# Token rows of a grouped mixture of experts: gathered by TensorE per block, or scattered to DRAM once per layer and read back

## What is computed

```
e_idx, wts = top-2 experts of the token's best group, weights normalised
dest  = position of each (token, expert) pair in a list that is sorted by
        expert and padded to whole blocks
xs    = h_pad[slot_tok].reshape(n_blocks, BLOCK, D)          # rows of one expert
def block_ffn(args):
    xb, e = args
    return (silu(xb @ w_gate[e]) * (xb @ w_up[e])) @ w_down[e]
ys    = lax.map(block_ffn, (xs, block_e))
out   = zeros(N + 1, D).at[slot_tok].add(ys * slot_w)[:N]
```

## Time and profile before

| | |
|---|---|
| runs | 1494.18, 1494.39, 1498.3 us; median 1494.39 |
| the profiled execution | 1502.44 us, its span 1500.3 us |
| TensorE busy | 1428.7 us, 95% of the span |
| VectorE, ScalarE, Pool busy | 45%, 16%, 7% |
| DMA, mean of the span | 335 GB/s; 409 or 410 in most slices of the expert loops |
| DMA queues | q1 (SyncE) 487.84 MB, 82.5% of 16 engines' span; q0 (Pool) 11.21 MB, 2.3% |
| granted clock, mean | 0.974 |

### The profile page before, as it was taken

One profiled execution on the slowest core, in us unless ns is written; L12 is line 12 of the kernel. 1 busy time (PEld: TensorE's weight loads), 2 busy tenths in 40 slices (PEclk: granted clock), 3 DMA queues, 4 the chain that ended last, 5 costly groups with the idle time before them and its releaser, 6 DMA issues.

```text
span 1500.3 us, 19677 instructions
## 1 busy us (share of the span) xinstructions
PE 1428.7 (95%) x6993; PEld 658.7 (44%) x6994; DVE 682.3 (45%) x1986; ACT 239.8 (16%) x392; POOL 104.6 (7%) x149
## 2 busy tenths in 40 slices
PE   6999998999999999999989999999999999999996
PEld 2777664333333233333347766633333333333333
DVE  2697647333323333343338965553333323233333
ACT  1201322111111011111130122211111101111112
POOL 1071111000000000000002511100000000000000
PEclk9899998999999999999999999889999999999998
DMA  9944558999999985899998265589999999979991
GB/s 335 352 175 151 209 204 322 410 409 410 409 410 410 409 321 223 309 410 410 409 409 331 112 242 210 192 330 393 410 410 409 410 409 410 409 299 409 410 410 72
DMA packets 131317, 501.98 MB, mean 335 GB/s; under 512 B 8635, under 2 KB 8955, under 8 KB 131266
## 3 DMA queue, kind: packets, MB, share of 16 engines
q1 hardware_dynamic: 127056, 487.84, 82.5%
q0 software_dynamic: 3600, 11.21, 2.3%
q10 hardware_dynamic: 626, 2.46, 0.6%
HBM read 495.32 MB, written 7.00 MB: 335 GB/s over the span
## 4 chain that ended last, share of the span: by engine, by line
PE 60%; SPq 25%; DMA 5%; DVE 4%; issue 3%; ACT 2%; PEld 1%; PEldq 1%; ACTq 0%; DVEq 0%
PE ps L414 57%; SPq L380 18%; SPq L376 4%; PE ps L417 3%; DMA ring<-in_w_mod 2%; DMA ring<-in_w_exp_up 2%; SPq L396 1%; SPq L318 1%; PEld ps L414 1%; ACT hT L866 1%; ACT arena L866 1%; ACT L866 0%; SPq L382 0%; DVE stat L1053 0%; PEldq L563 0%
## 5 line engine op out<-in xcount | busy, mean ns | idle before, releaser
L414 PE MATMUL ps<-ring,arena 128*64 128x512 f32 x2816 | 635.7, 599 | 16.9 <-DMA ring<-in_w_exp_up 13.8
L414 PEld LDWEIGHTS ps<-ring,arena 128*64 128x64 f32 x2816 | 194.9, 137 | 404.7 <-issue 356.0
L866 ACT ACTIVATE arena<-ps 128x512 f32<-128x512 f32 (+3 forms) x240 | 129.6, 551 | 1124.8 <-PE ps L414 1033.9
L414 PE MATMUL ps<-arena 64*128 64x288 f32 (+4 forms) x1484 | 296.3, 505 | 12.0 <-DVE arena L1383 4.7
L414 PE MATMUL ps<-hT,ring 128*128 128x288 f32 x1024 | 257.9, 414 | 8.4 <-DVE hT L1127 4.1
L1416 DVE SCALAR_TENSOR_TENSOR xT<-ps,mod,xT 128x256 f32<-128x256 f32 x280 | 133.4, 476 | 267.7 <-PE ps L414 267.7
L414 PEld LDWEIGHTS ps<-hT,ring 128*128 128x128 f32 x1024 | 197.8, 194 | 66.4 <-issue 6.9
L414 PEld LDWEIGHTS ps<-arena 64*128 64x128 f32 (+4 forms) x1484 | 119.6, 161 | 203.0 <-issue 180.2
L1158 DVE SCALAR_TENSOR_TENSOR arena<-arena,wcT 128x256 f32<-128x256 f32 x240 | 123.5, 575 | 1.6
L1450 DVE TENSOR_TENSOR arena<-ps,arena 128x512 f32<-128x512 f32 x35 | 24.2, 692 | 195.9 <-PE ps L414 195.9
L417 PE MATMUL ps<-cst,arena 128*128 128x128 f32 (+5 forms) x533 | 83.0, 289 | 12.2 <-DVE arena L1040 7.2
(11 more groups left out here) (173 smaller groups left out, 628.3 us busy)
## 6 DMA issues: line engine op xcount, KB each, us to landing
ring<-in_w_exp_up SPq DMA_DIRECT2D x128, 1024.0 KB, 18.0
ring<-in_w_exp_down SPq DMA_DIRECT2D x128, 1024.0 KB, 17.7
ring<-in_w_exp_gate SPq DMA_DIRECT2D x64, 1024.0 KB, 17.8
ring<-in_w_mod SPq DMA_DIRECT2D x48, 1024.0 KB, 8.9
arena<-in_w_exp_gate SPq DMA_DIRECT2D x32, 1024.0 KB, 17.1
ring<-in_w_in SPq DMA_DIRECT2D x24, 1024.0 KB, 21.4
big<-in_w_exp_gate SPq DMA_DIRECT2D x16, 1024.0 KB, 18.2
hT<-in_w_exp_gate SPq DMA_DIRECT2D x16, 1024.0 KB, 18.4
```

Of the source, the lines that this page charges most:

```text
L414: return nc.tensor.matmul(out, lhsT, rhs, start=start, stop=stop, skip_group_check=True)
L866: return nc.scalar.activation(out, in_, f, **kw)
```

## The change

- A tensor in DRAM, `block_rows`, of 1664 rows x 1024 is added, and zeroed once, in the first layer, by one Pool DMA of 6.8 MB out of the still zero tile qm. VectorE waits for it before it first writes qm.
- Once per layer, after the row numbers, VectorE casts them to integers (rowi), and Pool issues six indirect DMAs (three token tiles, two experts a token) that put each token's row at its two places. Pool waits until all have landed, and for gt0_done, and then reads block 1's rows with two DMAs of 64 rows x 2 KB. All this stands ahead of the history load, of Pool's waits and drains, and so of `mix_open`.
- In the loop Pool issues the two reads of the next block as soon as TensorE has transposed the rows before them (xg_trans).
- TensorE loses the gather in the loop, ScalarE the copy of its result, VectorE sel, sel1 and their sum. The first block of a layer is still gathered.
- The fourth combining pair goes from the up product, and the third from the gate product, to the place after the transposes of hs, ahead of the down product; their PSUM banks change. VectorE takes them after it has copied the transposed hs. After the last block the old banks and order remain.
- The transposes are in another order: rows first (now after up, waiting for the DMA), then selw, then hs.

```diff
+XROWS = -(-(MAXBLK + 1) * BLK // P) * P
...
-        PAIR_BANKS = ((6, 7), (0, 5), (1, 4), (0, 5))
+        PAIR_BANKS = ((6, 7), (0, 5), (5, 7), (2, 3))
+        LAST_BANKS = ((6, 7), (0, 5), (1, 4), (0, 5))
...
                                 if k == 3:
                                     pe.wait_ge(V.y_copied, nn)
                                     pe.wait_ge(V.selT_copied, nn)
-                                    for j in range(3):
+                                    for j in range(2):
                                         combine(j).then_inc(V.comb_done, 1)
...
-                                if k == 0:
-                                    pe.wait_ge(V.comb_used, taken)
-                                    combine(3).then_inc(V.comb_done, 1)
...
-                            pe.wait_ge(V.sel_ready, nn)
-                            pe.reg_add(taken, taken, 1)
+                            pe.reg_add(got, got, 32)
+                            pe.wait_ge(V.rows_in, got)
+                            transposes(1, xtok).then_inc(V.xg_trans, 1)
+                            pe.wait_ge(V.selw_ready, nn)
+                            pe.reg_add(taken, taken, 2)
                             pe.wait_ge(V.comb_used, taken)
-                            gather().then_inc(V.gathered, 1)
-                            pe.wait_ge(V.h_act, nn)
-                            transposes(4, hs).then_inc(V.trans_done, 1)
-                            pe.wait_ge(V.selw_ready, nn)
                             for t, (t0, m) in enumerate(TILES):
                                 last = tr(ps[:, 6, t0:t0 + m], selw[0:m, t, :], m)
                             last.then_inc(V.selT_done, 1)
-                            pe.wait_ge(V.xrow_copied, nn)
-                            transposes(1, xtok).then_inc(V.xg_trans, 1)
+                            pe.wait_ge(V.h_act, nn)
+                            transposes(4, hs).then_inc(V.trans_done, 1)
+                            for j in range(2, 4):
+                                combine(j).then_inc(V.comb_done, 1)
...
+                v.tensor_copy(rowi[:, :, :], slots[:, :, :]).then_inc(V.rowi_ready, 1)
...
+                if l == 0:
+                    zeros = qm[:, :, :].rearrange("p h w -> p (h w)")
+                    pool.dma_start(xrows.rearrange("(p r) d -> p r d", p=P),
+                                   zeros.unsqueeze(1).to_broadcast([P, XROWS // P, D])).then_inc(rows_zeroed, 16)
...
+                pool.wait_ge(V.h2_copied, 6)
+                pool.wait_ge(V.rowi_ready, 1)
+                for t, (t0, m) in enumerate(TILES):
+                    for k in range(2):
+                        gp.indirect_dma_start(xrows[:, :], bass.IndirectOffsetOnAxis(ap=rowi[0:m, k, t:t + 1], axis=0),
+                                              h2tok[0:m, t, :], None).then_inc(rows_out, 16)
+                pool.wait_ge(rows_out, 96 * (l + 1))
+                pool.wait_ge(V.gt0_done, 1)
+
+                def read_rows(r0):
+                    for nh in range(2):
+                        pool.dma_start(xtok[nh * BLK:(nh + 1) * BLK, :], xrows[bass.ds(r0, BLK), nh * 512:nh * 512 + 512]) \
+                            .then_inc(V.rows_in, 16)
+
+                read_rows(BLK)
...
                 pool.drain().then_inc(mix_open, 1)
+                nb = pool.value_load(nsubi[0:1, E:E + 1], min_val=E, max_val=MAXBLK)
+                with pool.Fori(1, nb) as n:
+                    pool.wait_ge(V.xg_trans, n)
+                    pool.sem_inc(tick, 1)
+                    read_rows(n * BLK + BLK)
```

More of the change, by code:

```diff
@@ L145, in hybrid_step_kernel @@
         nsubi = sb("nsubi", [P, E + 1], i32)
+        rowi = sb("rowi", [P, 2, 3], i32)
+        xrows = nc.dram_tensor("block_rows", (XROWS, D), f32, kind="Internal").ap()
         rtmp = sb("rtmp", [P, KC, NS])
@@ L224, in hybrid_step_kernel @@
         sel = cut("moe", 3, BLK)
-        sel1 = cut("moe", 3, BLK)
         selw = cut("moe", 3, 2 * BLK)
@@ L420, in _ @@
             taken = pe.alloc_register("chunks_taken")
+            got = pe.alloc_register("rows_in_x32")
             for s in range(NSLOT):
@@ L741, in half_products, with combine @@
                     return last
-                def combine(j):
+                def combine(j, banks=PAIR_BANKS):
                     for hf in range(2):
-                        last = mm(ps[:, PAIR_BANKS[j][hf], 0:T], ysb[hf * 64:hf * 64 + 64, j * P:(j + 1) * P],
+                        last = mm(ps[:, banks[j][hf], 0:T], ysb[hf * 64:hf * 64 + 64, j * P:(j + 1) * P],
                                   selT[hf * 64:hf * 64 + 64, :], True, True)
@@ L756, in _ @@
                 pe.reg_mov(nn, 0)
-                pe.reg_mov(taken, 2)
+                pe.reg_mov(taken, 0)
+                pe.reg_mov(got, 0)
                 with pe.Fori(0, E // 2) as e2:
@@ L825, in _ @@
                             last.then_inc(V.down_done, 1)
+                            pe.reg_add(taken, taken, 2)
+                            pe.wait_ge(V.comb_used, taken)
+                            pe.sem_inc(tick, 1)
                 pe.reg_add(nn, nn, 1)
@@ L1427, in _ @@
                     last.then_inc(V.bchain, 1)
-                    dve.wait_ge(V.bchain, n * 3 + 1)
+                    dve.wait_ge(V.bchain, n * 2 + 1)
                     v.tensor_tensor(selw[:, :, :], selw[:, :, :], selw1[:, :, :], ALU.add).then_inc(V.selw_ready, 1)
                     v.tensor_scalar(slots[:, :, :], slots[:, :, :], -float(BLK), None, ALU.add).then_inc(V.bchain, 1)
-                    dve.wait_ge(V.bchain, n * 3 + 2)
-                    for t in range(3):
-                        v.tensor_scalar(sel[:, t, :], iota[:, 0:BLK], slots[:, 0, t:t + 1], None, ALU.is_equal)
-                    for t in range(3):
-                        last = v.tensor_scalar(sel1[:, t, :], iota[:, 0:BLK], slots[:, 1, t:t + 1], None, ALU.is_equal)
-                    last.then_inc(V.bchain, 1)
-                    dve.wait_ge(V.bchain, n * 3 + 3)
-                    v.tensor_tensor(sel[:, :, :], sel[:, :, :], sel1[:, :, :], ALU.add).then_inc(V.sel_ready, 1)
-                    for j in range(3):
+                    for j in range(2):
                         dve.wait_ge(V.comb_done, n * 4 + j + 1)
@@ L1444, in _ @@
                     v.tensor_tensor(hs, ps[:, 2, :], gs, ALU.mult).then_inc(V.gated, 1)
-                    dve.wait_ge(V.comb_done, n * 4 + 4)
-                    take(3)
                     dve.wait_ge(V.up_done, n + 1)
@@ L1452, in _ @@
                     v.tensor_copy(h2T, ps[:, 4, :]).then_inc(V.hT_copied, 1)
+                    for j in range(2, 4):
+                        dve.wait_ge(V.comb_done, n * 4 + j + 1)
+                        take(j)
                     dve.wait_ge(V.selT_done, n + 1)
+                    dve.wait_ge(V.bchain, n * 2 + 2)
                     v.tensor_copy(selT, ps[:, 6, 0:T]).then_inc(V.selT_copied, 1)
@@ L1569, in _ @@
                     pool.dma_start(dstate(rets_v, h), state(h)).then_inc(V.states_stored if i < 2 else V.Sa_stored, 16)
+                if l == 0:
+                    pool.wait_ge(rows_zeroed, 16)
+                pool.wait_ge(V.h2_copied, 6)
[11 more added lines that the diff above has]
+                read_rows(BLK)
                 pool.wait_ge(V.sf_stored, 16)
```

18 lines of the change are left out of this document (8 added, 10 removed).

## The result

The changed kernel takes 1539.8 us (median of 4 runs, 1535.2 to 1544.0) against 1496.4 us for the kernel before beside it (4 runs, 1494.2 to 1503.2): a ratio of 1.0281, 95% interval 1.0235 to 1.0328. The direction is the predicted one. The size is not: 1518 was forecast, and the upper end of the range, 1538, lies 2 us under the first median.

A forecast was written before the change was run, and what follows sets the result against it. The weight stream was taken to bound the kernel except in double experts. Gate delay and reads less TensorE's gain, with 5.0 us of lead spent at the end, gave +12.2 and +12.0, together +24 on 1494.4: 1518 us, range 1504 to 1538.

The forecast's parts named there:

- What bounds the kernel: Expert loop: one expert's weights take 30.7 us, one TensorE block 27.7; TensorE is slower only where an expert has two blocks.
- TensorE's block: Expert loop: gather and moved combining pairs cut a TensorE-paced block from 27.73 to 25.0 us, 2.7 less.
- What that is worth: Double experts only: TensorE's saving gives 9.2 us in the first layer and 3.8 us in the second.
- The reads: Expert loop: each block's 256 KB of rows costs the weight stream 0.8 us, upper end 1.3.
- Which blocks pay: Expert loop: reads cost time in 13 blocks of the first layer and 14 of the second; the others fall in idle stream.
- The scatter: Ahead of `mix_open`: scatter, landing wait and reads open the gate 12 us later in each layer; bounds 7 and 22.
- Hidden: Scratch zeroing, 16.6 us of DMA at 50 to 93 us, is covered; so is block 1's wait of some 2 us.
- C: Half-rate reads in the loop: 1.3 instead of 0.8 us a block, 27 times, +14, 1532 us; chance 0.12.
- rival B: Slow scatter ahead of the gate: 3 us per indirect DMA, gate 22 us late in each layer, 1538 us; chance 0.10.
- A: The forecast itself, gate delay and reads less TensorE's gain: 1518 us; chance 0.66.
- D: No change: the gate opens when it does now and a read costs 0.65 us, 1490 to 1496 us; chance 0.05.
- E: Faster: gate as now, and reads filling gaps between the weights' packets cost the stream nothing, 1473 us; chance 0.04.

The follow-up runs named there:

- pairs_only: The kernel before with only the two combining pairs moved; TensorE still gathers every block, no scratch, scatter or reads: ratio to before 1.0001.
- no_reads: The changed kernel with block rows never read back, Pool raising the semaphore itself; only the first layer is comparable: 477.9 us against 497.4.
- pairs_scatter: The kernel before with the two combining pairs moved, plus zeroing and scatter ahead of the gate, nothing read back: 1509.6 us, ratio to before 1.0081.
- after: The changed kernel itself, against the kernel before: 1539.8 us, ratio 1.0281.
- reads_inter: The changed kernel with block rows read by one DMA over all 128 partitions from a contiguous source, ScalarE's copy restoring order: 1514.8 us, ratio to before 1.0114.
- reads_twice: The changed kernel with each block's rows read a second time into a tile nobody reads: 1584.7 us.
- gate_first: The changed kernel with the scatter, its wait and the first read moved behind Pool's signal mix_open: 1545.8 us.
- before: The kernel without the change: 1496.4 us beside the changed kernel, 1498.0 to 1498.9 beside the experiments.

## Why the prediction was wrong

By its own steps:

- **What bounds the kernel: right.** Weights pace single-block experts; TensorE's saving came back in the double ones and hardly elsewhere. pairs_only and the waits above show it.
- **TensorE's block: right in the sum.** 24.81 against 25.0. In its parts the moved pairs bring 0.2 us (0.4 by my terms, 1.21 + 0.42 - 0.85 - 0.38), and the gather more.
- **What that is worth: a little low.** -9.2 was forecast for the first layer; no_reads minus pairs_scatter gives -12.2 (0.9 of it is a signal that stands earlier, 3.3 instead of 2.4 us before the first product), the pairs another -0.8. I had counted three blocks at TensorE's pace and a part; in no_reads five periods of 24.81 us follow one another (560 to 684 us).
- **The reads: the step that failed.** I took 0.8 us a block, from the earlier trace rows, and 1.3 as the upper end. In single-block experts it is 1.3, and by layers 19.5 us for the first against 10.4 forecast. A read over all partitions costs 0.61 us a block, and 487.6 - 477.9 = 9.7 us in that layer. So the row's 0.8 was somewhat high for the transfer that the row shows (all partitions), and far too low for the one that the change makes (half of them); that 9.7 is near 10.4 is luck, a lower price on more blocks. The prediction also says of the earlier trace rows that Pool's 1.47 MB take no more of the engines than their bytes; the row has 4.4 us of all engines where the bytes at 410 GB/s are 3.6. And the rows travel in packets of 4 KB, 64 a read, not of 2 KB. For the second layer after minus pairs_scatter is +17.2, against 11.2 - 3.8 = 7.4 forecast; 12.4 of it go with whole-width reads (after minus reads_inter), and 2.4 are a later signal (3.6 instead of 6.0 us before the first product; 0.6 of them are in the 12.4 too).
- **Which blocks pay: too few.** I let 27 of 35 pay. reads_twice shows 1.4 us on nearly all of them.
- **The scatter: right in form, too large in the first layer.** An issue took 0.86 to 1.06 us (1.3 forecast), and Pool went on 2.2 us after the first layer's last issue had ended, where 7.1 was forecast from the stores in the earlier trace rows: the stream that those landed beside has run dry by then (share 0.45; beside a full one, in gate_first, it was 11.5). The drain is held up by the loads under way, as forecast (6.1 us, ending 1.4 after the landing). The signal's delays of 8.4 and 13.1 us stand against 12 and 12. Where they were tried alone, in pairs_scatter, they were worth 8.4 and 7.7, against 11 (12 - 1) and 4.6 (12 - 2.4 - 5.0) forecast.
- **Hidden: right** for the zeroing; block 1's wait for its rows never showed in after (24.81 us from the first product to the second).
- **The sum.** 24 were forecast. The two layers gave 38.8 (+14.9, +23.9), of which the first divides by runs: gate +8.4, reads +19.5, gather -12.2, pairs -0.8. These are differences of a chain of runs from before to after, so they must add up; in another order of the edits the shares could differ. In the second the gate is 7.7 + 2.4, the pairs -1.0, and 14.8 are left for the reads less TensorE's gain; with the forecast gain of 3.8 the reads cost 18.6. By this estimate the reads are 38.1 against 21.6 forecast, 16.5 too few; all other terms together were 2 too many, and the layers' sum missed by 38.8 - 24.2 = 14.6.
- **The range.** C had a chance of 0.12 and gave 1532. It stood on a median of 1494.4 from three runs, while the three sets of before beside the experiments have medians of 1498.0 to 1498.9: 1536 on that base. The top of the range, 1538, was rival B by itself; half-rate reads together with a base 4 us higher and a gate only a few microseconds dearer were left out, though none of the three excludes the others.

Rival by rival: A failed by the size of the reads; B by the issues, 0.96 us at the median, at most 1.06. Its second ground was not put to the test: VectorE's routing was over before the first issue, which waits for it (row numbers cast at 244.1, issue at 245.2), and the six issues take 1.06 to 0.86 us in the same order in gate_first, where VectorE does little beside them, as in after, where it works beside the first three. C is what happened; D and E needed cheap reads and an early gate, and after has neither.

## What to carry to other kernels

A row is near in the property that sets the cost, or it isn't near: for a DMA beside a full stream ask which partitions it fills before how many bytes it brings. Two DMAs that fill 64 partitions each, one after the other, cost this full-rate stream twice their bytes (1.3 us for 262 KB beside 410 GB/s); the same bytes over all partitions, by one DMA or by two interleaved ones, cost them once. And work taken from an engine that isn't the bound (here 2.9 us of TensorE a block) is worth only the stretches where it was, while what replaces it is paid in every block.

## What the runs showed that I had not expected

- A full-busy share of the DMA engines (1.00 to 1.04) does not mean full rate: 254 GB/s stood beside it.
- A read whose source address has a register and three dimensions was cut into 448 packets of 8 bytes beside 64 of 4 KB, and 256 KB took 16 us from issue to landing instead of 5.8.
- Indirect stores of up to 128 rows of 4 KB cost Pool 0.86 to 1.06 us to issue, about as much as a plain store of its state tiles (0.89).
- Pool's drain lasts until 1.0 to 1.4 us after the last of its own loads has landed (in after 255.7 + 4.7 = 260.4 for the history load, 255.7 + 6.1 = 261.8 for the drain; in before 253.45 and 254.49), and 1.6 us with nothing under way.
- After 15.6 us without work TensorE started again at a granted clock of 0.50 (gate_first), so a long wait for one DMA costs more than its own length.
